# Two-block model kernel: 160 instead of 144 expert tokens through indirect DMAs, with three moves of small work around it

## The reference, cut to what matters

```python
def peer(xn, w_q, sub_keys, u_tab, v_tab):
    ...
    q = (t @ w_q).reshape(n_tok, PEER_HEADS, 2, PEER_HALF)
    sc = jnp.einsum("thpk,hpnk->thpn", q, sub_keys).astype(jnp.float32)
    s_top, i_top = lax.top_k(sc, PEER_TOPK)
    cand = s_top[:, :, 0, :, None] + s_top[:, :, 1, None, :]
    ...
    best, pos = lax.top_k(cand.reshape(n_tok, PEER_HEADS, kk), PEER_TOPK)
    idx = jnp.take_along_axis(cand_idx.reshape(n_tok, PEER_HEADS, kk), pos, axis=-1)
    g = jax.nn.softmax(best, axis=-1).astype(xn.dtype)
    ...
        act = jax.nn.gelu(jnp.einsum("phkd,pd->phk", ue, tb))
        return jnp.einsum("phk,phkd->pd", gb * act, ve)
```

```python
    log_f = jax.nn.log_sigmoid((f_logit + b_f).astype(jnp.float32))
    c = jnp.cumsum(log_f, axis=1).transpose(0, 2, 1)
```

## Time and profile before

| | us |
|---|---|
| median of 3 runs | 1638.59 (1638.20 to 1638.82) |
| the profiled execution, whole | 1639.54 |
| its span (first to last instruction) | 1637.7 |
| PE busy | 1617.2 (99%) |
| DVE busy | 1273.7 (78%) |
| ACT busy | 925.9 (57%) |
| POOL busy | 317.9 (19%) |
| granted PE clock, mean | 0.998 |

### The profile page before, as it was taken

How to read it: one execution, slowest core, us unless ns; L and a number is a source line. 1 busy time by engine, 2 the same in 40 slices (tenths; PEclk the granted TensorE clock), 3 DMA queues, 4 the chain that set the end, 5 groups by cost and what they waited for, 6 DMA issues and landing times.

```text
span 1637.7 us, 29003 instructions
## 1 busy us (share of the span) xinstructions
PE 1617.2 (99%) x10027; PEld 1437.5 (88%) x10027; DVE 1273.7 (78%) x2416; ACT 925.9 (57%) x1571; POOL 317.9 (19%) x193
## 2 busy tenths in 40 slices
PE   9999999999999999999999999999999999999998
PEld 8999899999988888888888888988888888788886
DVE  7888878987988887666666667678777876687777
ACT  5776655455566665555555555665555545555554
POOL 1000002878788880000000000010000000000000
PEclk9999999999999999999999999999999999999999
DMA  7766766776777775777777786446666654356663
GB/s 237 237 233 228 257 196 190 174 177 168 186 176 162 162 166 167 219 220 220 220 219 219 220 256 207 148 136 191 186 190 188 208 149 147 118 179 185 188 188 107
DMA packets 126803, 312.09 MB, mean 191 GB/s; under 512 B 35200, under 2 KB 53376, under 8 KB 126336
## 3 DMA queue, kind: packets, MB, share of 16 engines
q1 hardware_dynamic: 101664, 296.02, 59.3%
q0 software_dynamic: 23328, 9.52, 4.7%
q10 hardware_dynamic: 1728, 5.45, 1.0%
HBM read 298.78 MB, written 11.62 MB: 190 GB/s over the span
## 4 chain that ended last, share of the span: by engine, by line
PE 82%; issue 7%; DVE 6%; DMA 2%; ACT 2%; POOL 0%; POOLq 0%; DVEq 0%; SPq 0%; ACTq 0%
PE ps L1293 16%; PE ps L1323 9%; PE ps L1325 9%; PE ps L1327 9%; PE ps L1295 8%; PE ps L1273 8%; PE ps L1275 8%; PE ps L1274 8%; PE ps L1439 2%; PE ps L1306 1%; DVE low L1747 1%; DVE held_low L1747 1%; DVE arena L1816 0%; PE ps L1414 0%; DMA raw<-in_w_query 0%
## 5 line engine op out<-in xcount | busy, mean ns | idle before, releaser
L1747 DVE TENSOR_TENSOR low<-raw,high 128x1024 fp32r<-128x1024 f32 (+1 forms) x516 | 621.4, 1210 | 126.4 <-ACT high L869 124.7
L869 ACT ACTIVATE high<-raw 128x1024 fp32r<-128x1024 f32 (+1 forms) x517 | 538.6, 1045 | 271.9 <-PE ps L1275 134.5
L1293 PE MATMUL ps<-x_parts,high 128*128 128x512 f32 x1184 | 423.1, 400 | 0.0
L1273 PE MATMUL ps<-x_parts,low 128*128 128x256 f32 x1328 | 377.9, 285 | 0.9 <-DVE x_parts L1863 0.9
L1274 PE MATMUL ps<-x_parts,high 128*128 128x256 f32 x1328 | 375.7, 283 | 0.0
L1275 PE MATMUL ps<-x_parts,high 128*128 128x256 f32 x1328 | 375.7, 283 | 0.0
L1295 PE MATMUL ps<-x_parts,low 128*128 128x256 f32 x1184 | 332.3, 281 | 0.0
L793 POOL DMA_INDIRECT routed<-h_tok,subln x128 | 255.4, 1995 | 121.5 <-DVE h_tok L2137 67.4
L1293 PEld LDWEIGHTS ps<-x_parts,high 128*128 128x128 f32 x1184 | 222.5, 188 | 53.0
L1273 PEld LDWEIGHTS ps<-x_parts,low 128*128 128x128 f32 x1328 | 254.8, 192 | 2.7 <-issue 1.0
L1274 PEld LDWEIGHTS ps<-x_parts,high 128*128 128x128 f32 x1328 | 254.8, 192 | 0.0
(11 more groups left out here) (363 smaller groups left out, 1779.9 us busy)
## 6 DMA issues: line engine op xcount, KB each, us to landing
raw<-in_u_tab SPq DMA_DIRECT2D x128, 512.0 KB
raw<-in_v_tab SPq DMA_DIRECT2D x128, 512.0 KB
raw<-in_ffn_in SPq DMA_DIRECT2D x88, 512.0 KB
raw<-in_w_mix SPq DMA_DIRECT2D x56, 512.0 KB
raw<-in_ffn_out SPq DMA_DIRECT2D x44, 512.0 KB
routed<-arena POOLq DMA_DIRECT2D x18, 512.0 KB, 4.2
h_tok<-routed SPq DMA_DIRECT2D x128, 72.0 KB, 3.4
raw<-in_w_query SPq DMA_DIRECT2D x16, 512.0 KB
```

What stands on the lines that cost most here:

```text
L869: a.activation(w_high(p, 0, n), cols(raw, p, 0, n), ACT.Copy).then_inc(slot_high[p.slot], 1)
L1273: pe.matmul(dst, left[1], right[0], start=start, stop=False)
L1293: pe.matmul(bank(b).rearrange("p (h t) -> p h t", h=2), cols(high, p, k * PARTS, PARTS), both[:, :, k, :], start=(k == 0), stop=False)
L1747: v.tensor_tensor(w_low(p, 0, n), cols(raw, p, 0, n), w_high(p, 0, n).bitcast(F32), ALU.subtract).then_inc(slot_low[p.slot], 1)
```

## The change

`EXTRA` goes from 16 to 32, so `ROUTED` from 144 to 160, `GROUPS` from 28 to 24, `SPREAD` from 8 to 4, and `OF_HEAD` from 2 to 4 (32 extra DMAs instead of 16). The table grows to 20 parts of 512 KB, and the parts above 16 are cleared in the first four rounds of the mixer instead of after it. Round 0 of the top-16 is made as two calls, token tile 0 and then token tile 1, with every second low part in each; POOL may start after the first. ACT gets a second exponential in that round. The low part of `fox_v` piece 5 is made within the log chain.

```diff
-EXTRA = 16
+EXTRA = 32
-ZERO_PARTS = 18
+ZERO_PARTS = 20
...
+        def weighed_until(p):
+
+            return sum(groups_until(q) > 0 for q in range(p))
...
-                    sp.wait_ge(chosen_ready, ROUNDS)
+                    sp.wait_ge(chosen_ready, ROUNDS + 1)
...
                 pool.dma_start(cleared[2 * c + 1], zeros).then_inc(zeroed, 16)
-            for n in range(2 * KC, ZERO_PARTS):
-                pool.dma_start(cleared[n], zeros).then_inc(zeroed, 16)
+                if c < ZERO_PARTS - 2 * KC:
+                    pool.dma_start(cleared[2 * KC + c], zeros).then_inc(zeroed, 16)
...
-                    pool.wait_ge(chosen_ready, h // 2 + 1)
+                    pool.wait_ge(chosen_ready, h // 2 + 2 if h else 1)
...
+                    if k == OF_ROUND // 2 - 1:
+                        a.wait_ge(shifted_ready, 1)
+                        w = slot_weight[:, 0, 0:32]
+                        a.activation(w, w, ACT.Exp).then_inc(exp_ready, 1)
                     if k % OF_ROUND == OF_ROUND - 2:
-                        a.wait_ge(shifted_ready, it + 1)
-                        w = slot_weight[:, :, 32 * it:32 * it + 32]
+                        a.wait_ge(shifted_ready, it + 2)
+                        w = slot_weight[:, :, 32 * it:32 * it + 32] if it else slot_weight[:, 1, 0:32]
                         a.activation(w, w, ACT.Exp).then_inc(exp_ready, 1)
...
-            def log1p_of_exp(dst, e, t):
+            def log1p_of_exp(dst, e, t, piece=None):
...
-                link(v.tensor_scalar(dst, z2, 1.0 / 15.0, None, ALU.mult))
+                chain.step(v.tensor_scalar(dst, z2, 1.0 / 15.0, None, ALU.mult))
+                if piece:
+                    ahead(piece)
+                chain.wait()
...
-            for it in range(ROUNDS):
+            def top_k(it, bs):
...
+                def low_between(n):
+                    if len(bs) == TB:
+                        ahead(u[n])
+                    elif n % 2 == 1:
+                        ahead(u[n // 2 + OF_ROUND // 2 * bs[0]])
...
+            for it in range(ROUNDS):
+                for q in range(0 if it else 2, 4):
+                    ahead(piece_query(4 * it + q))
+                v.wait_ge(sc_ready, it + 1)
+                if it == 0:
+                    top_k(it, (0,))
+                    top_k(it, (1,))
+                else:
+                    top_k(it, (0, 1))
...
-                    if p > LEAD:
-                        v.wait_ge(pair_weighed, p - LEAD)
+                    if weighed_until(p):
+                        v.wait_ge(pair_weighed, weighed_until(p))
...
-                    log1p_of_exp(log_gate, gate_e, (gate_t2, gate_t3))
+                    log1p_of_exp(log_gate, gate_e, (gate_t2, gate_t3), Piece("fox_v", 1))
...
-                    ahead(Piece("fox_v", 1))
```

More of the change, by code:

```diff
@@ L2033, in best_of @@
                 return t[:, m * 16 + 8 * n:m * 16 + 8 * n + 8]
-            for it in range(ROUNDS):
+            def top_k(it, bs):
                 u = [piece_u(it * OF_ROUND + i) for i in range(OF_ROUND)]
-                for q in range(0 if it else 2, 4):
-                    ahead(piece_query(4 * it + q))
+                rounds_done = it + (bs[-1] if it == 0 else 1)
+                tiles = [(b, q) for b in bs for q in range(4)]
+                pairs = [2 * b + h for b in bs for h in range(2)]
+                of_pairs = slice(2 * bs[0], 2 * bs[-1] + 2)
+                of_tiles = slice(bs[0], bs[-1] + 1)
+                heads = slice(32 * it, 32 * it + 32)
+                def low_between(n):
[3 more added lines that the diff above has]
+                        ahead(u[n // 2 + OF_ROUND // 2 * bs[0]])
                 def scores(b, q):
@@ L2047, in next_eight @@
                     return ins
-                v.wait_ge(sc_ready, it + 1)
+                third = len(tiles) * 3 // 8
                 for b, q in tiles:
@@ L2052, in _ @@
                 chain.step(ins)
-                ahead(u[0])
+                low_between(0)
                 chain.wait()
[L2055 to L2061, removed]
+                next_eight(tiles[0:third])
+                low_between(1)
+                next_eight(tiles[third:2 * third])
+                low_between(2)
+                next_eight(tiles[2 * third:]).then_inc(sc_used, 1)
+                low_between(3)
+                v.wait_ge(sc_used, rounds_done + 1)
                 for b, q in tiles:
@@ L2114, in _ @@
                     chain.wait()
-                    chain.step(v.tensor_tensor(eqs4, eqs4, idx4[:, :, n, :].unsqueeze(2).to_broadcast([PARTS, 4, 16, 16]), ALU.mult))
+                    chain.step(v.tensor_tensor(eqs4[:, of_pairs], eqs4[:, of_pairs],
+                                               idx4[:, of_pairs, n, :].unsqueeze(2).to_broadcast(shape), ALU.mult))
                     if n == 0:
-                        ahead(u[13])
+                        low_between(13)
                     chain.wait()
-                    chain.step(v.tensor_reduce((slot_i, slot_j)[n][:, :, heads], by_place, AX.X, ALU.add))
+                    chain.step(v.tensor_reduce((slot_i, slot_j)[n][:, of_tiles, heads], by_place[:, of_tiles], AX.X, ALU.add))
@@ L2120, in _ @@
                 chain.wait()
-                chain.step(v.tensor_scalar(first_place[:, 0:32], slot_i[:, 0, heads], float(ROUTED), token, ALU.mult, ALU.add))
-                chain.step(v.tensor_scalar(first_place[:, 32:64], slot_i[:, 1, heads], float(ROUTED), token_extra, ALU.mult, ALU.add))
-                v.wait_ge(exp_ready, it + 1)
-                sums = expsum[:, 0:4]
-                link(v.tensor_reduce(sums.rearrange("p (b h) -> p b h", b=TB), weights4, AX.X, ALU.add))
+                for b in bs:
+                    chain.step(v.tensor_scalar(first_place[:, 32 * b:32 * b + 32], slot_i[:, b, heads], float(ROUTED),
+                                               (token, token_extra)[b], ALU.mult, ALU.add))
@@ L2135, in _ @@
-                chain.step(ins)
-                chain.wait()
-                v.tensor_copy(extra_weight[:, of_round], slot_weight[:, 1, heads].rearrange("p (n q) -> p n q", q=SPREAD)).then_inc(chosen_ready, 1)
-                ahead(u[15])
+                for b in bs:
+                    chain.step(v.tensor_tensor(weights4[:, b], weights4[:, b],
+                                               expsum[:, 2 * b:2 * b + 2].unsqueeze(2).to_broadcast([PARTS, 2, 16]), ALU.mult))
+                if 1 in bs:
+                    v.scalar_tensor_tensor(out=extra_index[:, of_round], in0=slot_j[:, 1, heads].rearrange("p (n q) -> p n q", q=SPREAD),
+                                           scalar=float(PARTS * ROUTED), in1=first_place[:, 32:64].rearrange("p (n q) -> p n q", q=SPREAD),
+                                           op0=ALU.mult, op1=ALU.add)
+                    chain.wait()
+                    ins = v.tensor_copy(extra_weight[:, of_round], slot_weight[:, 1, heads].rearrange("p (n q) -> p n q", q=SPREAD))
```

71 lines of the change are left out of this document (36 added, 35 removed).

## The result

The changed kernel takes 1643.77 us (median of 7 runs, 1640.89 to 1646.18), the kernel before 1638.48 beside it (7 runs). The ratio is 1.003, 95% interval 1.002 to 1.004: slower by 0.3%, where 1634.0 had been forecast, and outside the range. The profiled execution of after took 1644.24, its span is 1642.4; before's span is 1637.7, so +4.7 is to be explained.

A forecast was written before the change was run, and what follows sets the result against it. PE, busy 1617.2 of 1637.7 us, was taken as the bound. Groups -3.4 and fox -1.2 sum to -4.6, all else 0: 1639.54 becomes 1634.9 profiled, median 1634.0, range 1632.8 to 1638.6.

The forecast's parts named there:

- Groups: PE's mask groups in the inner pairs: 28 to 24, each worth 0.85 us, -3.4 in all (3.0 to 3.5).
- Fox: Low part of fox_v piece 5 made earlier: PE's 1.24 us wait goes, no new wait, -1.2.
- Round 0: Top-16 in two calls on DVE, 23.1 us each with lows: cost 0, up to +2.5 at the upper bound.
- Clearing: Two more 512 KB table parts, three clearing DMAs per mixer round boundary instead of two: 0 (0 to +1).
- POOL's start: Extra indirect DMAs start at 466 (465.5 to 470), held until the repacked entries land.
- POOL's end: Last of 80 indirect DMAs landed at 640.4, bounds 637.8 to 647; cost 0, at the bounds 0 to +5.5.
- mean of two counts: POOL's 80 DMAs: end at 641.2 by the 2.19 mean, 636 by slow DMAs per group; middle 638.6 taken.
- The price of being late: Outer-stage start: PE feels nothing until SP is released about 2.4 us after the last group, at 641.5.
- rival 1: POOL late before the outer stage, landing at 643 to 649: PE loses 1.5 to 7.5, 1635.5 to 1641; chance 0.15.
- rival 2: POOL far too late at 2.72 per DMA: PE stands 44 us, 1678, slower from 649.4 on; chance 0.06 in any degree.
- margin of 1.1 us: Ahead of the outer stage: POOL's last landing at 640.4 against 641.5, when PE would feel SP's release.
- two-port case for the one-hots: Inner pairs: DVE's one-source one-hots block GpSimd's descriptor writing, matching the 2.54 us DMAs; would support 636 over 641.2.

The follow-up runs named there:

- run 1: Kernel before with only the low part of fox_v piece 5 moved into the log chain: 1636.86 us against 1638.69, ratio 0.9987.
- run 3: Kernel before with only round 0 of the top-16 made in two calls: 1638.61 us, ratio 0.9999.
- run 7: Kernel after with the four table parts above 16 cleared behind the second RMS norm's inverse roots instead of in the mixer: 1641.26 us, ratio 1.0014 to before.
- run 4: Kernel after with the four extra table parts cleared just behind the mixer instead of within it: 1647.73 us, ratio 1.0056 to before.
- run 6: Kernel after with head 5's own 16 DMAs ahead of the wait for the packed weights, extras in later heads: 1639.07 us, ratio 1.0002 to before.
- run 9: Kernel after with the mask groups' one-hots written by an instruction that reads two tensors: 1644.52 us, ratio 1.0036 to before.
- run 10: Kernel after with the 24 groups in consecutive pairs, 6 to 29: 1643.32 us, ratio 1.0032 to before.
- run 8: Kernel after with head 5's own DMAs first and the four parts cleared behind the inverse roots: 1636.58 us, ratio 0.9982 to before.
- run 11: Kernel after with the low parts of the inner pieces written in two halves: 1635.36 us, ratio 0.9975 to before.
- run 12: Kernel after with clearing behind the inverse roots, head 5's own DMAs first and inner low parts in halves: 1631.40 us, ratio 0.9957 to before.

## Why the prediction was wrong, step by step

Two steps failed. POOL's pace was taken to go by the groups, 172.6 us for 80 DMAs; it took 179.0, because a low part that is under way holds a DMA up. And the clearing was put at 0 and cost 2.7. With both, SP was 8.2 us behind the last group, and PE paid 5.9 us of waiting and 2.6 at half clock where 0 was forecast.

- **Groups, -3.4 forecast: right in kind, undersized.** The four pairs gave 4.2, 1.04 each. The earlier trace rows compare pairs of the end of the stage, with the step into the next stage in them, so they made a pair without a group look dearer than it is.
- **Fox, -1.2 forecast: right.** -1.5 in the trace of after, -1.8 in run 1. The rest of the chain, one low part later, was waited for by nobody.
- **Round 0, 0 forecast: right.** A call took 23.25 us where 23.1 was worked out (231.16 to 254.41 in after), and run 3 shows no cost.
- **Clearing, 0 (0 to +1) forecast: wrong, +2.7.** The step that failed took a stretch at a DMA share of 0.88 with PE fully busy as proof that there is room. The mean share didn't even rise: from 0.73 to 0.72 over 24 to 196. My reading is that a burst against the few loads in flight counts; no run shows how the queues share the engines. Run 7 gives the cost back by another place, run 4 only moves it.
- **POOL's start, 466 forecast: 468.55.** Of these 2.5 us the repacked load's issue is 1.5 (464.88 instead of 463.34), since PE's work ahead of it had slipped; the other 1.0 is the load itself, which took 3.7 to land where 466 allows it 2.7.
- **POOL's end, 640.4 forecast: 649.1.** This step failed most: of the 8.7 us the pace is 6.4 (179.0 for the 80 instead of 172.6), the start 2.5 (the last landing took 0.3 less). The pace was taken as the mean of two counts: 21 slow DMAs, one for each group, or before's mean of 2.19. There were 29 in 80 over 2.2 us, and 2.24 each, because these have nothing to do with groups: a low part that is under way holds POOL up, and the pairs without a group that the change makes are where every DMA meets one (513.74, 516.59 and 519.37 in after, 2.54, 2.47 and 2.57 long). The row of the slow DMA in the earlier trace rows (505.42) was read against the wrong neighbour on DVE. The one-hots lie in a slow DMA's span; the low part lies at its beginning (in before it ran from 505.33 to 506.55, and 506.55 - 505.42 - 0.12 = 1.01 is what that DMA took more). The prediction's own list said that it would be wrong outright if the pace depended on something other than the groups.
- **The price of being late.** The forecast let SP come 2.4 us behind the last group before PE feels it. In after SP's first table part is 8.2 behind the group's end (640.50 + 0.39, 649.11), and 8.2 - 2.4 = 5.8 stands beside a wait of 5.93; in run 6 it is 6.2 and 4.0. In runs 4, 7, 9 and 10 SP is 8.2 to 8.3 behind as well and PE waits 6.6 to 6.8, in run 8 6.0 and 4.45: there the slack is 1.5 to 1.6. What differs is the load of v2. ACT's high of v2 never waits for it in after (655.07, 6.0 behind SP's first table part) and 0.2 in run 6; in the five others it waits 0.8 to 1.1 and starts 6.9 to 7.0 behind. The prediction had both loads there after 4.1 + 1.3 = 5.4, the 1.3 without a row. So this step held to within 0.9 us. But rival 1 and 2 priced only the wait. The half clock behind it was left out: 2.6 us here, of 8.5 in all nearly a third, and 1.4 to 2.6 in the seven profiled kernels in which PE waited there.
- **Which case came.** It lies where rival 1 passes into rival 2: SP went on at 649.1, and rival 2 decides from 649.4 on; with the half clock and the clearing added the result is slower. Rival 2 had been given 0.06, and rival 1, the same mechanism with less of it, 0.15. For a margin of 1.1 us with an uncertainty of 5 on POOL's side that was far too little.

The Trainium skill (SBUF — State Buffer, "Who interferes with whom") says that a VectorE instruction with two SBUF inputs contends with a GpSimd instruction that reads the SBUF, and that one with at most one such input, outside the two-port modes, doesn't. The traces agree: the low part has two inputs in the SBUF and holds, the reduction from PSUM has none there and doesn't. But the same section of the Trainium skill also says that in a probe `tensor_tensor` did not stall a DMA; here it holds up the issue of an indirect one, 33 times in after. The Trainium skill gives on the same page (SBUF — State Buffer, "A bandwidth-pool intuition that's wrong") the block, measured beside a `tensor_copy`, as lasting until VectorE's end plus about 115 ns. No such addition shows here: a held DMA takes 1.54 plus what is left at +0.12, to within 0.03, and so ends 1.42 behind VectorE's end. The prediction cited this page's two-port case for the one-hots. In after they never lie where a DMA can be held, so it wasn't at work there; in runs 11 and 12 it may be, for 14 DMAs and some 0.9 us in all.

What stays open: why four 512 KB writes delay the mixer's loads by so much when two don't reach PE (how the queues share the DMA engines wasn't tried), what lets the load of v2 land about 1 us earlier in after than in run 7, and what run 4 lost beyond its trace.

## What to carry to other kernels

Before laying an engine's slow instructions to a cause, line up every one of them with what the other engines do at its start, not over its span, and ask the same of the instructions that took their normal time: what is present there too isn't the cause. Where GpSimd issues many indirect DMAs beside VectorE's two-input work, cut that work in pieces or expect GpSimd to fall in step with it; halving 64 instructions at 0.06 us each bought 8.4 us of the program here, where POOL's end was what PE waited for. And price a wait of PE of several us with the time at half clock behind it, where the profile shows PEclk at 0.50 after such waits.

## What the runs showed of the hardware that I had not expected

- An indirect DMA of 128 entries takes POOL 1.54 us and a gap of 0.30, and up to 1.03 more when a VectorE operation on two SBUF tiles began before it and is under way 0.12 us behind its start; 33 of 33 in after and 422 of 422 in all traces, within 0.03 us. One that began within 0.03 us of the DMA's start held none of 16.
- POOL gets its turn between the two halves of a low part issued back to back (1.91 us for a DMA that met the first half).
- After 4.0 to 6.8 us without matmuls at the outer start, PE's matmuls ran at half clock (0.50 in 658 to 662 of after); it cost 2.6 us in after and 1.4 to 2.6 in the six other kernels with such a wait.
- Twenty 512 KB writes from POOL's queue, in the mixer's first four rounds in threes instead of twos, made ACT's waits for weight loads grow from 2.1 to 27.7 us while the mean DMA share of that stretch stayed at 0.72 to 0.73.
